# The long convolutions' transforms taken over mirrored halves of the tokens

## The chip, the cores and the metric

The kernel runs on one core of a Trainium2 chip. A time is the device time of one execution in microseconds (us). The core has TensorE (products and transposes, into PSUM), VectorE, ScalarE and GpSimd (elementwise work), and SyncE (SP), which here only issues the transfers from memory. Each engine runs its own list of instructions in order, and they meet at semaphores: an instruction can wait until a semaphore has reached a number, and raises one when it is done.

## The reference

Two transformer blocks in sequence for 256 tokens of width 1024: the first with two layers (a pooling mixer and a stick-breaking attention, each with a gated feed-forward part), the second with one layer, whose mixer has two branches, an attention over a neighbourhood and a pair of long convolutions. The change is in the convolutions alone:

```python
def long_conv_bidir(u, h_fwd, h_bwd, bias):
    B, L, C = u.shape
    k2 = jnp.concatenate([h_fwd, jnp.zeros((1, C), jnp.float32), h_bwd[:0:-1]], axis=0)
    U = jnp.fft.rfft(u.astype(jnp.float32), n=2 * L, axis=1)
    K = jnp.fft.rfft(k2, n=2 * L, axis=0)
    y = jnp.fft.irfft(U * K[None], n=2 * L, axis=1)[:, :L]
    return (y + u.astype(jnp.float32) * bias.astype(jnp.float32)).astype(u.dtype)

def hyena_mixer(hv, hx1, hx2, conv_w, conv_b, w1, b1, w2, b2, freq, w3, bias):
    u = short_conv(jnp.concatenate([hv, hx1, hx2], axis=-1), conv_w, conv_b)
    parts = jnp.split(u, HY_ORDER + 1, axis=-1)
    z, gates = parts[0], parts[1:]
    filt = hyena_filters(z.shape[1], w1, b1, w2, b2, freq, w3)
    for n in range(HY_ORDER):
        z = gates[n] * long_conv_bidir(z, filt[:, 0, n], filt[:, 1, n], bias[n])
    return z
```

Here L is 256, the width 512, and there are two convolutions in a row. All is float32.

## The kernel before

**How numbers are multiplied.** Every float32 operand of a product is split into a high and a low half (two tiles in the type float32r), and one product is three on TensorE: high by high, high by low, low by high (`mm3`). "Product" below means one of the three. For a weight tile (128 x 1024) ScalarE writes the high half (`high_halves`, L1690) and VectorE subtracts it from the tile for the low half (`low_halves`, L1002). The same pair of steps stands behind every intermediate result (`copy`, L1701, and `minus`, L1024).

**Weights.** SP loads tiles into a ring of six places; a tile's place is free when its low half is made. The halves lie in a ring of five. In the mixer, `used(n)`, written in the lists of ScalarE and VectorE, makes the halves of all tiles up to number n + 5. The order of the tiles is the list `MIX_TILES`: q0 to q3, h0 to h11 and g0 to g15, the tiles of queries, of the convolution branch and of the gates.

**The mixer's order.** It is written out by hand, once for each engine, as a list of calls. On TensorE (L850 to L920) gemms of 24 products of 256 columns (`q5`, `h_mm`, `g_mm`) stand between the attention of four pairs of heads (`na_scores`, `na_turn`, `na_attend`) and the convolution branch.

**The convolution branch.** After `h_mm(j)` ScalarE copies the result into a padded line and starts the short convolution (`h_step`), VectorE finishes it with two operations of 256 columns (`h_conv`, L1433 and L1435). For j from 0 to 7 TensorE turns the result (`h_rows`), so that tokens lie on partitions: j = 0 to 3 is the input u, 4 to 7 the first gate X1T; 8 to 11 is the second gate X2 and is not turned. `filter_tile` and `spectrum` make the filters' spectra, KS. Then, for n = 0 and 1, `transform(n)` on TensorE multiplies the 256 tokens by the cosine and the sine matrix, for each half `ft` of the frequencies and each part `c`: 2 x 2 results, each the sum over two blocks `t` of 128 tokens. VectorE multiplies them by the spectrum as complex numbers (`transform`, L1565 to L1573) and makes high and low halves with ScalarE. The way back is two more matrix products: the first return ("bt", 24 products of 512 columns) is multiplied by X1T (L1602) and becomes the input of the second transform; the second return ("bf", 48 products of 256 columns) is multiplied by X2 (L1615) and goes into the merge (`W_MIXO`), where the fourth block of the first tile waits for the last of it. One matrix serves both ways; `matrix_high` and `matrix_low` make its halves from the transfer `dft_s`.

**What stands around it.** On TensorE: `spectrum(1)`, h11, the first transform, g7, g8, g9, the first return, g10, the second transform, g11 to g14, the second return, g15, the merge. PSUM has eight banks, given out in turn; a bank waits until what it held last has been read. VectorE applies the first block's final norm to the residual (eight operations, L1609) after the second transform.

Of the kernel before, what the change touches and what calls it, by code (L numbers as in the profile page):

```python
# [13 lines left out]
KT = 8  # L14
# [45 lines left out]
def tables():  # L60
# [15 lines left out]
    a, b = np.arange(T1)[:, None], np.arange(T1)[None, :] + 0.5  # L76

    def pair(ang):
        m = np.stack([np.cos(ang), -np.sin(ang)]).astype(f32)
        return np.ascontiguousarray(m.reshape(2, 2, 128, T1).transpose(2, 0, 1, 3).reshape(128, 4 * T1))  # L80


    k = pair(2 * np.pi * a * b / 512)
    high = (k.view(np.uint32) & np.uint32(0xFFFFF000)).view(np.float32)
    o["dft_k"] = np.concatenate([high, k - high], axis=1)
    o["dft_s"] = pair(2 * np.pi * (a + 0.5) * b / 512)
# [99 lines left out]
def build(nc, T):  # L186
# [165 lines left out]
    def sems(names):  # L352
# [23 lines left out]
    mod_done, x2_u, x2_hi, x2_lo, k_cp, rope_dve, kx_hi, kx_lo, h_fin = sems(  # L376
        "mod_done x2_u x2_hi x2_lo k_cp rope_dve kx_hi kx_lo h_fin")
# [44 lines left out]
    def mix_w(step):  # L422
        return W_MIX + MIX_TILES.index(step)

# [4 lines left out]
    def tensor(pe):  # L429
# [303 lines left out]
        def h_rows(j):  # L733
            b = bank(("ht", j), u_lo if j < 4 else x1_cp, j % 4 + 1)
            pe.wait_ge(conv_done, 2 * j + 2)
            tr(pb(b, 128), f(CONV[j % 2], 128))
            tr(pb(b, 128, at=128), f(CONV[j % 2] + 128, 128)).then_inc(ht_mm, 1)
# [157 lines left out]
        pe.wait_ge(table_lo, 2)  # L895
        pe.wait_ge(u_lo, 4)
        transform(0)
        for m in range(7, 10):
# [8 lines left out]
        g_mm(10)  # L907
        pe.wait_ge(back_dve, 4)
        transform(1)
        for m in range(11, 15):  # L910
            g_mm(m)
        pe.wait_ge(dt_dve, 32)
        for j in range(4):
            b = bank(("bf", j), back_dve, 2 * j + 5)
# [1489 lines left out]
```

## Time and profile before

| | |
|---|---|
| three runs | 1004.68, 1004.76, 1005.01 us; median 1004.76 |
| the profiled execution | 1004.6 us, its span 1002.8 us |
| TensorE busy | 988.9 us, 99% |
| VectorE busy | 787.4 us, 79% |
| ScalarE busy | 556.5 us, 55% |
| granted TensorE clock | 0.998 of full on average |
| DMA | 188.02 MB, 186 GB/s read over the span |

Times within the program are counted from the span's start. Busy time of TensorE counts a product from its start to its modelled end, and products overlap, so the distance between starts says more. What the chain of waits shows is, at each step, the work that released the next. The kernel's first block ends at about 553 us, the second block's mixer runs to about 783 us, and the last feed-forward part to the end.

### The profile page before, as it was taken

The numbers are of one execution on the slowest core, as the hardware profiler recorded it, in microseconds if no ns is written. First come the engines' busy times: TensorE is split into PE (matmuls) and PEld (weight loads), VectorE is DVE, ScalarE is ACT, GpSimd is POOL, SyncE is SP. The second block draws the span as 40 slices with busy tenths as digits, with TensorE's granted clock in tenths as the row PEclk, the third lists the DMA queues.
The fourth block names the chain that finished last, engine by engine and source line by source line (L and its number), as shares of the span: only waits on it lengthen the run. The fifth ranks groups of instructions, "written<-read, shape, count | busy, mean of one in ns | idle before, by whom it ended". The sixth has DMA issues, their size and how long they took to land.

```text
span 1002.8 us, 19799 instructions
## 1 busy us (share of the span) xinstructions
PE 988.9 (99%) x7922; PEld 958.8 (96%) x7922; DVE 787.4 (79%) x1410; ACT 556.5 (55%) x932; POOL 23.1 (2%) x28
## 2 busy tenths in 40 slices
PE   9999999999999999999999999999999999999997
PEld 6999999999889999999999999999999999999997
DVE  5888889976899878989887776787788786766553
ACT  5654444444777665555454548795644565454442
POOL 4000000000000000000000000000001100000000
PEclk9999999999999999999999999999999999999999
DMA  8666667884443248886687414263334556555541
GB/s 307 217 207 225 213 216 252 288 313 145 137 132 123 95 136 316 312 271 231 212 277 248 153 43 137 100 214 130 120 108 161 181 187 204 171 192 175 162 147 42
DMA packets 53637, 188.02 MB, mean 187 GB/s; under 512 B 6120, under 2 KB 7689, under 8 KB 53034
## 3 DMA queue, kind: packets, MB, share of 16 engines
q1 hardware_dynamic: 53370, 186.17, 55.2%
q8 instruction: 63, 1.03, 0.4%
q10 hardware_dynamic: 176, 0.59, 0.2%
q14 instruction: 28, 0.23, 0.1%
HBM read 185.68 MB, written 1.05 MB: 186 GB/s over the span
## 4 chain that ended last, share of the span: by engine, by line
PE 80%; DVE 14%; ACT 3%; issue 2%; DMA 0%; DVEq 0%; POOL 0%; ACTq 0%; POOLq 0%
PE psum L445 79%; DVE memr L1002 5%; DVE memr L1024 2%; DVE memr L1209 1%; ACT memr L1690 1%; DVE mem L1206 1%; DVE mem L1200 1%; PE psum L460 1%; ACT mem L1701 1%; DMA mem<-in_w_up 0%; ACT mem L1832 0%; DVE psum L1191 0%; ACT memr L1701 0%; DVE mem L1166 0%; DVE psum L1453 0%
## 5 line engine op out<-in xcount | busy, mean ns | idle before, releaser
L445 PE MATMUL psum<-memr 128*128 128x256 f32 (+5 forms) x7666 | 957.3, 287 | 3.2 <-DVE memr L1024 1.3
L445 PEld LDWEIGHTS psum<-memr 128*128 128x128 f32 (+1 forms) x7666 | 930.6, 188 | 22.8 <-issue 7.4
L1002 DVE TENSOR_TENSOR memr<-mem,memr 128x1024 fp32r<-128x1024 f32 (+1 forms) x290 | 339.9, 1209 | 47.7 <-ACT memr L1690 47.5
L1690 ACT ACTIVATE memr<-mem 128x1024 fp32r<-128x1024 f32 (+2 forms) x296 | 290.8, 1026 | 13.2 <-DMA mem<-in_w_down 8.3
L1701 ACT ACTIVATE memr<-mem 128x256 fp32r<-128x256 f32 (+5 forms) x171 | 81.1, 484 | 282.3 <-DVE mem L1134 102.1
L1024 DVE TENSOR_TENSOR memr<-mem,memr 128x256 fp32r<-128x256 f32 (+3 forms) x129 | 59.6, 471 | 17.8 <-ACT memr L1701 16.8
L1119 DVE TENSOR_TENSOR mem<-psum,mem 128x256 f32<-128x256 f32 (+1 forms) x66 | 27.9, 423 | 42.3 <-PE psum L445 42.3
L1012 DVE CUSTOM_DVE_ANT_0 mem<-mem 128x1024 f32<-128x1024 f32 x48 | 58.6, 1221 | 0.6
L1698 ACT ACTIVATE mem<-mem 128x256 f32<-128x256 f32 (+1 forms) x56 | 22.9, 415 | 64.5 <-DVE mem L1657 32.4
L1024 DVE TENSOR_TENSOR memr<-psum,memr 128x256 fp32r<-128x256 f32 (+2 forms) x72 | 32.2, 462 | 13.5 <-ACT memr L1701 12.7
L1701 ACT ACTIVATE memr<-psum 128x256 fp32r<-128x256 f32 (+3 forms) x80 | 29.6, 404 | 7.8 <-PE psum L460 4.0
L1777 ACT ACTIVATE mem<-mem 128x256 f32<-128x256 f32 (+1 forms) x66 | 29.9, 452 | 7.0 <-DVE mem L1112 6.0
L460 PE MATMUL psum<-mem 128*128 128x128 f32 (+1 forms) x200 | 29.1, 276 | 3.4 <-DVE mem L1206 2.0
L460 PEld LDWEIGHTS psum<-mem 128*128 128x128 f32 (+1 forms) x200 | 21.6, 130 | 7.1 <-DVE mem L1206 2.5
L1112 DVE TENSOR_TENSOR mem<-psum,mem 128x256 f32<-128x256 f32 (+1 forms) x66 | 27.8, 421 | 0.1
L1701 ACT ACTIVATE mem<-psum 128x256 f32<-128x256 f32 (+2 forms) x55 | 22.3, 416 | 7.2 <-PE psum L445 6.9
L1701 ACT ACTIVATE memr<-psum,mem 16x512 fp32r<-16x512 f32 (+3 forms) x40 | 21.9, 595 | 6.9 <-PE psum L445 5.4
L1021 DVE TENSOR_TENSOR mem<-mem 128x256 f32<-128x256 f32 (+1 forms) x48 | 20.5, 427 | 4.7 <-ACT mem L1698 3.5
L1657 DVE SCALAR_TENSOR_TENSOR mem<-psum,mem 128x256 f32<-128x256 f32 x8 | 3.9, 484 | 23.3 <-PE psum L445 23.3
L1009 DVE CUSTOM_DVE_ANT_0 mem<-mem 128x1024 f32<-128x1024 f32 x16 | 19.5, 1220 | 1.4 <-ACT mem L1773 1.4
L445 PE MATMUL psum<-mem 128*128 128x512 f32 (+7 forms) x56 | 18.6, 456 | 1.7 <-POOL mem L2248 1.3
L1134 DVE TENSOR_TENSOR mem<-mem 128x272 f32<-128x272 f32 (+1 forms) x44 | 18.7, 425 | 0.3 <-ACT mem L1777 0.3
(132 smaller groups left out, 373.4 us busy)
## 6 DMA issues: line engine op xcount, KB each, us to landing
mem<-in_w_gate SPq DMA_DIRECT2D x66, 512.0 KB, 4.1
mem<-in_w_up SPq DMA_DIRECT2D x66, 512.0 KB, 4.5
mem<-in_w_ada SPq DMA_DIRECT2D x48, 512.0 KB, 4.6
mem<-in_w_down SPq DMA_DIRECT2D x48, 448.0 KB, 4.3
mem<-in_w_in SPq DMA_DIRECT2D x40, 512.0 KB, 4.4
mem<-in_w_down SPq DMA_DIRECT2D x24, 512.0 KB, 4.8
mem<-in_sb_qkv SPq DMA_DIRECT2D x24, 512.0 KB, 4.5
mem<-in_sb_o SPq DMA_DIRECT2D x8, 512.0 KB, 3.4
```

What stands on the lines that cost most here:

```text
L445: return pe.matmul(out, a, b, start=start, stop=stop)
L460: return pe.transpose(out, in_, ident[0:p, 0:p])
L1002: dve.tensor_tensor(r(ol, n), raw(e), rf(oh, n), ALU.subtract).then_inc(w_lo, 1)
L1012: dve.tensor_tensor_reduce(out=f(JUNK, 1024), in0=raw(e), in1=f(SILC, 1024), scale=1.0, scalar=0.0, op0=ALU.mult, op1=ALU.add, accum_out=f ...
L1021: dve.tensor_tensor(f(SQA, n), f(SQA, n), f(SQT[i % 2], n), ALU.add).then_inc(sq_add, 1)
L1024: return dve.tensor_tensor(out, x, hi, ALU.subtract)
L1112: last = dve.tensor_tensor(f(TT, n), pb(bg, n), f(RSTD, n), ALU.mult)
L1119: last = dve.tensor_tensor(f(UU, n), pb(bu, n), f(RSTD, n), ALU.mult)
L1690: act.activation(r(oh, n), raw(e), ACT.Copy).then_inc(w_hi, 1)
L1698: act.activation(f(SQT[i % 2] if i else SQA, n), x, ACT.Square).then_inc(sq_act, 1)
L1701: return act.activation(out, in_, ACT.Copy, bias=0.0, scale=scale)
L1777: act.activation(f(SSL, n), f(TT, n), ACT.Silu, bias=f(FCOL[k], 1) if shift else 0.0).then_inc(silu_done, 1)
```

## The change

The matrices of the transform are even or odd about the middle of the tokens, and for half of the frequencies and parts only the sum of a token and its mirror image counts, for the other half only the difference. The kernel now makes the sum and the difference (of 128 rows each) once, and each result of the transform takes one block in place of two. The frequencies are put in an order in which even ones come first. The first return gives an even part and an odd part of 128 rows, and the two halves of the tokens are their sum and their difference.

- `h_conv(j)`: for j < 4 an add and a subtract of 128 columns, of the first half and the reversed second half, into the padded line; for j 4 to 7 a reversed copy of the second half. `h_rows` turns these.
- TensorE: `transform(n)` has 12 products of 512 columns in place of 24, the first return 12 in place of 24.
- After the first return: ScalarE copies one part to SBUF; VectorE makes sum and difference, multiplies each by its part of X1T, and makes sum and difference again for the second transform.
- The matrix there and the matrix back are now different: `dft_f` (0.5 MB, already in halves) and `dft_i` (1 MB, in halves), loaded after `spectrum(1)`. ScalarE copies each into the type float32r, the second between the halves of the first transform; VectorE's `matrix_low` is gone.
- Order: on TensorE g10 now stands before the first return, g11 and g12 behind it, g13 to g15 before the second return. On VectorE the final norm stands before `h_conv(10)`, and the tiles of `used(24)` to `used(31)` are spread between other steps.

```diff
@@ tables
+    s = np.stack([np.cos(ang) + np.sin(ang), np.cos(ang) - np.sin(ang)]).astype(f32)
+    o["dft_f"] = halves(s[:, :128].transpose(1, 0, 2).reshape(128, 2 * T1))
+    o["dft_i"] = halves(s.reshape(2, T1, 2, 128).transpose(3, 0, 2, 1).reshape(128, 4 * T1))
...
@@ TensorE
+        def forward(c, ft):
+            o = MATR + 256 * c + 128 * ft
+            return r(o, 128), r(o + 512, 128)
+
+        def inverse(c, ft, n):
+            o = 512 * c + 256 * ft
+            return r(MATH + o, n), r(MATL + o, n)
...
                     b = bank(("dt", n, ft, c), dt_dve, 16 * n + 8 * ft + 2 * c + 2)
-                    for t in range(2):
-                        last = mm3(pb(b), *mat(c, t, 128 * ft, 128), r(UH + 512 * t, 512), r(UL + 512 * t, 512), t == 0, t == 1)
-                    last.then_inc(dt_mm, 1)
+                    t = (c + ft) % 2
+                    mm3(pb(b), *forward(c, ft), r(UH + 512 * t, 512), r(UL + 512 * t, 512), True, True).then_inc(dt_mm, 1)
...
-        for t in range(2):
-            b = bank(("bt", t), back_dve, 2 * t + 1)
+        pe.wait_ge(table_hi, 5)
+        for t in (1, 0):
+            b = bank(("bt", t), *((back_dve, 2), (back_cp, 1))[t])
             for c in range(2):
-                for ft in range(2):
-                    last = mm3(pb(b), *mat(c, ft, 128 * t, 128), *y_of(c, ft, 0, 512), c + ft == 0, c + ft == 2)
+                ft = (c + t) % 2
+                last = mm3(pb(b), *inverse(c, ft, 128), *y_of(c, ft, 0, 512), c == 0, c == 1)
             last.then_inc(back_mm, 1)
@@ VectorE
+            if j < 4:
+                early, late = f(CONV[k], 128), f(CONV[k] + 128, 128)[:, ::-1]
+                dve.wait_ge(conv_done, c + 2)
+                dve.tensor_tensor(f(PADB[k] + 1, 128), early, late, ALU.add).then_inc(conv_done, 1)
+                dve.tensor_tensor(f(PADB[k] + 129, 128), early, late, ALU.subtract).then_inc(conv_done, 1)
+            elif j < 8:
+                dve.wait_ge(conv_done, c + 2)
+                dve.tensor_copy(f(PADB[k] + 129, 128), f(CONV[k] + 128, 128)[:, ::-1]).then_inc(conv_done, 1)
...
+        z, x = ([f(SPARE[k] + 512 * t, 512) for t in range(2)] for k in range(2))
+        dve.wait_ge(back_mm, 2)
+        dve.wait_ge(back_cp, 1)
+        for t, op in enumerate((ALU.add, ALU.subtract)):
+            dve.tensor_tensor(z[t], pb(bank_of["bt", 0]), x[0], op).then_inc(back_dve, 1)
+        for t in range(2):
+            dve.wait_ge(back_dve, t + 1)
+            dve.tensor_tensor(z[t], z[t], f(X1T + 512 * t, 512), ALU.mult).then_inc(back_dve, 1)
+        dve.wait_ge(back_dve, 4)
+        for t, op in enumerate((ALU.add, ALU.subtract)):
+            dve.tensor_tensor(x[t], z[0], z[1], op).then_inc(back_dve, 1)
...
             dve.tensor_tensor(z, pb(bank_of["bf", j], T1), f(X2 + T1 * j, T1), ALU.mult).then_inc(back_dve, 1)
+            if j < 3:
+                used(29 + j)
@@ ScalarE
+        transform(0, 0)
+        act.wait_ge(dft_in, 48)
+        copy(r(MATH, 2048), f(MATH, 2048)).then_inc(table_hi, 1)
+        gate(7)
+        used(24)
+        transform(0, 1)
...
@@ SP
-        sp.dma_start(f(MATR, 1024), T["dft_s"]).then_inc(dft_in, 16)
+        sp.dma_start(f(MATR, 1024), T["dft_f"]).then_inc(dft_in, 16)
+        raws(W_MIX + 30)
+        sp.wait_ge(sp_mm, 8)
+        sp.dma_start(f(MATH, 2048), T["dft_i"]).then_inc(dft_in, 16)
```

TensorE before, from the third gate behind the first transform (g9) through the first return and g10 to the start of the second transform (x23 and x5 are the rest of a gemm or a result):

```order
L445 MATMUL psum<-memr 128x256 [waits ks_done,w_lo]
L445 MATMUL psum<-memr 128x256 x23
L445 MATMUL psum<-memr 128x512 [waits h_cp,dt_dve]
L445 MATMUL psum<-memr 128x512 x11
L445 MATMUL psum<-memr 128x512 [waits dt_dve]
L445 MATMUL psum<-memr 128x512 x11
L445 MATMUL psum<-memr 128x256 [waits dt_dve,w_lo]
L445 MATMUL psum<-memr 128x256 x23
L445 MATMUL psum<-memr 128x512 [waits dt_dve,back_dve]
L445 MATMUL psum<-memr 128x512 x5
```

The same place after, from g10:

```order
L454 MATMUL psum<-memr 128x256 [waits h_cp,w_lo]
L454 MATMUL psum<-memr 128x256 x23
L454 MATMUL psum<-memr 128x512 [waits dt_dve,table_hi]
L454 MATMUL psum<-memr 128x512 x5
L454 MATMUL psum<-memr 128x512 [waits dt_dve]
L454 MATMUL psum<-memr 128x512 x5
L454 MATMUL psum<-memr 128x256 [waits dt_dve,w_lo]
L454 MATMUL psum<-memr 128x256 x23
L454 MATMUL psum<-memr 128x256 [waits dt_dve,w_lo]
L454 MATMUL psum<-memr 128x256 x23
L454 MATMUL psum<-memr 128x512 [waits gate_act,back_dve]
L454 MATMUL psum<-memr 128x512 x2
```

The return has half the products, and two gemms stand between it and the second transform in place of one.

VectorE before, from the end of the first transform to the start of the second (L1002 are weight tiles, L1602 the product by the gate, L1024 low halves):

```order
L1024 TENSOR_TENSOR memr<-mem,memr 128x512 [waits y_hi] x2
L1002 TENSOR_TENSOR memr<-mem,memr 128x1024 [waits w_hi] x3
L1602 TENSOR_TENSOR mem<-psum,mem 128x512 [waits back_mm,x1_cp]
L1024 TENSOR_TENSOR memr<-mem,memr 128x512 [waits back_hi]
L1602 TENSOR_TENSOR mem<-psum,mem 128x512 [waits back_mm]
L1024 TENSOR_TENSOR memr<-mem,memr 128x512 [waits back_hi]
L1002 TENSOR_TENSOR memr<-mem,memr 128x1024 [waits w_hi]
```

The same place after:

```order
L1046 TENSOR_TENSOR memr<-mem,memr 128x512 [waits y_hi] x2
L1024 TENSOR_TENSOR memr<-mem,memr 128x1024 [waits w_hi] x2
L1633 TENSOR_TENSOR mem<-psum,mem 128x512 [waits back_cp,back_mm,x1_cp]
L1633 TENSOR_TENSOR mem<-psum,mem 128x512
L1636 TENSOR_TENSOR mem<-mem 128x512 [waits back_dve] x2
L1639 TENSOR_TENSOR mem<-mem 128x512 [waits back_dve]
L1639 TENSOR_TENSOR mem<-mem 128x512
L1046 TENSOR_TENSOR memr<-mem,memr 128x512 [waits back_hi] x2
L1024 TENSOR_TENSOR memr<-mem,memr 128x1024 [waits w_hi]
```

Eight operations stand where four stood, with one weight tile fewer ahead of them, and none of them can begin before both results are there.

VectorE after, at the third convolution tile (L1455 and L1458 are the convolution, L1462 and L1463 the two new ones) and the weights of the attention behind it:

```order
L1455 SCALAR_TENSOR_TENSOR mem<-mem 128x256 [waits h_cp]
L1458 SCALAR_TENSOR_TENSOR mem<-mem 128x256 [waits conv_done]
L1462 TENSOR_TENSOR mem<-mem 128x128 [waits conv_done]
L1463 TENSOR_TENSOR mem<-mem 128x128
L1046 TENSOR_TENSOR memr<-psum,memr 128x512 [waits pt_hi] x4
```

Before, the convolution's second operation is followed at once by the four of the attention.

## Rows read from the trace of the kernel before

**Rows 1.** The page, busy us, share of the span and instructions of an engine.
```profile
PE 988.9 (99%) x7922; PEld 958.8 (96%) x7922; DVE 787.4 (79%) x1410; ACT 556.5 (55%) x932; POOL 23.1 (2%) x28
```

**Rows 2.** The chain of waits, 726 to 1003 us: start, length, what.
```profile
726.28 267.78 PE psum L445 x2214
```

**Rows 3.** The chain of waits, 626 to 670 us.
```profile
647.73 0.48 DVE mem L1435
648.21 1.10 DVE memr L1024 x2
...
663.29 0.50 DVE mem L1433
663.81 0.49 DVE mem L1435
...
665.89 0.48 DVE mem L1435
...
669.40 0.71 PE psum L445 x2
```

**Rows 4.** TensorE's weight loads in order of time, 640 to 670 us.
```profile
653.14 1.49 PEld L445 LDWEIGHTS psum<-memr 64*128 64x128 f32 x24 [0.37 <-DVE memr L1024]
...
661.03 2.89 PEld L445 LDWEIGHTS psum<-memr 128*128 128x128 f32 x24 [0.31 <-DVE memr L1002]
```

**Rows 5.** Products by shape, 726.2 to 731.7 us: busy us, mean ns, idle.
```profile
L445 PE MATMUL psum<-memr 128*128 128x512 f32 x24 | 5.7, 395 | 0.0
```

**Rows 6.** TensorE by stretch: us, busy (starts counted), granted clock, DMA share, GB/s.
```profile
711.98:717.58 5.60, 5.60 (x26) 1.00 0.56 189
717.58:725.98 8.40, 8.40 (x74) 1.00 0.18 63
```

**Rows 7.** VectorE in order of time, 600 to 640 us: start, us.
```profile
628.77 2.48 DVE L1024 TENSOR_TENSOR memr<-psum,memr 128x512 fp32r<-128x512 f32 x4 [0.39 <-ACT memr L1701]
...
631.18 0.44 DVE L1401 STREAM_SHUFFLE mem<-mem 128x256 f32<-128x256 f32 x1
631.51 0.42 DVE L1404 TENSOR_TENSOR mem<-mem 128x256 f32<-128x256 f32 x1
631.84 0.42 DVE L1406 TENSOR_TENSOR mem<-mem 128x256 f32<-128x256 f32 x1
```

**Rows 8.** VectorE by shape, whole span.
```profile
L1206 DVE TENSOR_TENSOR mem<-mem 128x144 f32<-128x144 f32 x16 | 4.5, 284 | 0.0
```

**Rows 9.** VectorE in order of time, 705 to 735 us.
```profile
710.70 1.23 DVE L1024 TENSOR_TENSOR memr<-mem,memr 128x1024 fp32r<-128x1024 f32 x1 [4.52 <-ACT memr L1701]
...
716.16 0.68 DVE L1565 TENSOR_TENSOR mem<-psum,mem 128x512 f32<-128x512 f32 x1
716.77 0.68 DVE L1566 TENSOR_TENSOR mem<-psum,mem 128x512 f32<-128x512 f32 x1
...
721.16 0.68 DVE L1565 TENSOR_TENSOR mem<-psum,mem 128x512 f32<-128x512 f32 x1
...
730.33 0.69 DVE L1602 TENSOR_TENSOR mem<-psum,mem 128x512 f32<-128x512 f32 x1
731.72 0.69 DVE L1024 TENSOR_TENSOR memr<-mem,memr 128x512 fp32r<-128x512 f32 x1 [0.70 <-ACT memr L1701]
```

**Rows 10.** VectorE in order of time, 750 to 762 us.
```profile
754.18 3.25 DVE L1609 SCALAR_TENSOR_TENSOR mem<-mem 128x256 f32<-128x256 f32 x8
757.35 0.41 DVE L1615 TENSOR_TENSOR mem<-psum,mem 128x256 f32<-128x256 f32 x1
758.24 0.42 DVE L1024 TENSOR_TENSOR memr<-mem,memr 128x256 fp32r<-128x256 f32 x1 [0.48 <-ACT memr L1701]
```

**Rows 11.** ScalarE in order of time, 670 to 725 us.
```profile
671.65 1.98 ACT L1701 ACTIVATE memr<-mem 128x2048 fp32r<-128x2048 f32 x1
...
724.27 1.23 ACT L1701 ACTIVATE memr<-mem 128x512 fp32r<-128x512 f32 x2 [3.75 <-DVE mem L1571]
```

**Rows 12.** DMA issues, 640 to 800 us: KB each, median us to landing.
```profile
mem<-in_dft_k SPq DMA_DIRECT2D x1, 1024.0 KB, 6.9
```

More of the change, by code:

```diff
@@ L423, in mix_w, with convolved @@
         return W_MIX + MIX_TILES.index(step)
+    def convolved(j):
+        return 2 * (j + 1) + min(j + 1, 4) + min(j + 1, 8)
     bank_of = {}
@@ new lines, in transform @@
+        def transform(n, ft):
+            base, c = (SPARE, [PX[0], PX[2]])[ft], 16 * n + 8 * ft
+            t1, t2, t3, t4 = f(base[0], 512), f(base[0] + 512, 512), f(base[1], 512), f(base[1] + 512, 512)
+            kre, kim = f(KS[n] + 1024 * ft, 512), f(KS[n] + 1024 * ft + 512, 512)
+            br, bi = bank_of["dt", n, ft, 0], bank_of["dt", n, ft, 1]
+            dve.wait_ge(ks_done, 4 * n + 4)
+            dve.wait_ge(dt_mm, 4 * n + 2 * ft + 1)
+            dve.tensor_tensor(t1, pb(br), kre, ALU.mult).then_inc(dt_dve, 1)
+            dve.tensor_tensor(t3, pb(br), kim, ALU.mult).then_inc(dt_dve, 1)
+            dve.wait_ge(dt_mm, 4 * n + 2 * ft + 2)
+            dve.tensor_tensor(t2, pb(bi), kim, ALU.mult).then_inc(dt_dve, 1)
+            dve.tensor_tensor(t4, pb(bi), kre, ALU.mult).then_inc(dt_dve, 1)
+            dve.wait_ge(dt_dve, c + 3)
+            dve.tensor_tensor(t1, t1, t2, ALU.subtract).then_inc(dt_dve, 1)
+            dve.wait_ge(dt_dve, c + 4)
+            dve.tensor_tensor(t3, t3, t4, ALU.add).then_inc(dt_dve, 1)
+            for i, x in enumerate((t1, t3)):
+                o = YB + 1024 * i + 512 * ft
+                dve.wait_ge(y_hi, 4 * n + 2 * ft + i + 1)
+                minus(r(o + 2048, 512), x, rf(o, 512)).then_inc(dt_dve, 1)
@@ L1590, in vector @@
         used(20)
+        for i in range(KT):
+            dve.scalar_tensor_tensor(hx(i, NMETA, T1), hx(i, NMETA, T1), vec("final_norm", i), f(SROOT, T1),
+                                     ALU.mult, ALU.mult)
         h_conv(10)
-        matrix_low()
         used(22)
@@ L2190, in scalar @@
         used(22)
-        matrix_high()
+        act.wait_ge(dft_in, 32)
+        copy(r(MATR, 1024), f(MATR, 1024)).then_inc(table_hi, 1)
         spectrum(1)
@@ L2194, in scalar @@
         used(23)
-        transform(0)
-        for m in range(7, 10):
-            gate(m)
-            used(17 + m)
+        transform(0, 0)
+        act.wait_ge(dft_in, 48)
+        copy(r(MATH, 2048), f(MATH, 2048)).then_inc(table_hi, 1)
+        gate(7)
+        used(24)
+        transform(0, 1)
+        gate(8)
+        used(25)
+        gate(9)
+        used(26)
+        gate(10)
+        act.wait_ge(back_mm, 1)
+        copy(f(SPARE[1], 512), pb(bank_of["bt", 1])).then_inc(back_cp, 1)
         for t in range(2):
-            act.wait_ge(back_dve, 2 * t + 1)
+            act.wait_ge(back_dve, t + 5)
             act.wait_ge(dt_mm, 4)
-            copy(r(UH + 512 * t, 512), f(SPARE[t], 512)).then_inc(back_hi, 1)
-        gate(10)
+            copy(r(UH + 512 * t, 512), f(SPARE[1] + 512 * t, 512)).then_inc(back_hi, 1)
         used(27)
-        transform(1)
-        for m in range(11, 15):
-            gate(m)
-            used(17 + m)
+        gate(11)
+        gate(12)
+        transform(1, 0)
+        used(28)
+        gate(13)
+        gate(14)
+        transform(1, 1)
+        gate(15)
         for j in range(4):
-            act.wait_ge(back_dve, 2 * j + 5)
+            if j < 3:
+                used(29 + j)
+            act.wait_ge(back_dve, 2 * j + 9)
             copy(r(YHYH + T1 * j, T1), f(SPARE[j % 2] + T1 * (j // 2), T1)).then_inc(back_hi, 1)
-        gate(15)
         used(32)
```

126 lines of the change are left out of this document (49 added, 77 removed).

## The prediction, on record before the changed kernel ran

> **What bounds the kernel now.** I read the page's first part, then busy time by stretch, then the chain of waits, then each engine in order of time around the change. The page has TensorE busy for 99% of the span and VectorE for 79% [rows 1]. A busy TensorE is not proof that it sets the time, so the reader is to look at where it stops. The chain of waits after the first return is one unbroken piece of TensorE: 2214 products in 267.78 us, from 726.28 to 994.06 us [rows 2]. There, a product that is left out shortens the program by the distance between two products, and any new stop adds its full length. Before 670 us it is otherwise. The chain runs over VectorE and ScalarE for some 40 us and comes to TensorE only at 669.40 [rows 3], and TensorE's weight loads stand idle 0.37 and 0.31 us for VectorE on the way [rows 4]. So two parts of the change fall on different ground: the products fall where TensorE binds, and the folding operations fall where VectorE binds.
>
> **Products removed.** Each transform has 12 products of 512 columns in place of 24, and so does the first return; the second return keeps its 48 of 256 columns. That is 3 x 12 = 36 products. The price is the distance from start to start, not the 395 ns for which one stands busy [rows 5]: in the stretch of the first transform 26 of them (two are of 256 columns, at its edges) take 5.60 us, so 24 take 24 x 0.233; 72 of 256 columns take 8.40 us, 0.117 each, with two edge records [rows 6]. The two prices stand as 2 to 1, as the columns do. 36 x 0.233 = 8.4 us off TensorE.
>
> The Trainium skill, page "TensorE: Matmul & The Clock Gate", section "Back-to-back issue gap", says that a sustained stream of 512-column products with their weight loads runs at about 131 ns each. By that rule 36 of them would be worth 4.7 us, an estimate from the page. The trace disagrees, 233 ns against 131.
>
> **Folding on VectorE (h_conv).** Tiles 0 to 3 get an add and a subtract of 128 columns, one operand read backwards, tiles 4 to 7 one backwards copy. No row has 128 such columns. Two starts of 256-column operations are 0.33 us apart (631.18, 631.51, 631.84 [rows 7]), two of 512 columns 0.61 (716.16 and 716.77 [rows 9]), so 128 columns come to about 0.20 us. A wait on the operation just before adds some 0.12: the second operation of a convolution, which waits for the first, starts 0.52 after it (663.29 and 663.81 [rows 3]), against 0.41 where eight of the same form follow each other (3.25 us [rows 10]). So a folded tile costs 0.12 + 2 x 0.20 = 0.52 us and a copied one 0.32. Bounds: nothing where VectorE waits anyway, and 0.61 per operation if a backwards read costs as much as 512 plain columns, which is the farthest row; the 144-column row (284 ns busy, against 0.42 to 0.44 at 256 [rows 7, 8]) is the nearest, and it fits 0.20 from start to start.
> Which of them count? Tile 0 and tile 1 come before waits for ScalarE; ahead of the weights of the second pair VectorE idles 0.39 us [rows 7], so tile 1 leaves about 0.13. Tile 2 (chain at 647.73, then straight into 648.21), tile 3 (663.81) and tile 4 (665.89) are on the chain [rows 3]: 0.52 + 0.52 + 0.32. Together 1.5 us, less about 0.15 for what the ends absorb: VectorE's last piece before 669.40 is 1.35 us later. TensorE, which waited there already, has nothing left to hide it. I take +1.35, between 0 (all hidden) and 4.3 (seven operations at 0.61, and the waits). Tiles 5 to 7 fall after 670 us, where VectorE is some microseconds ahead of TensorE: nothing.
>
> From here on I use the times of the trace; the shift of 1.35 goes on top of all.
>
> **First transform.** VectorE loses matrix_low (1.23 us at 710.70, after 4.52 us of idleness) and gets the eight final_norm operations, 3.25 us, into that idleness [rows 9, 10]: hidden. It can start the complex products at about 715.5 instead of 716.16; both halves take 10.1 (716.16 to 721.16 for one [rows 9]), so they end at 725.6. TensorE ends the transform 2.8 us earlier, but the gate g10 (2.8 us) has been put behind g9, so it arrives at the return at 726.0 as before. Slack 0.4 us, cost nothing. Between the halves ScalarE gets the 2048-column copy of the return's matrix, 1.98 us; it idles 3.75 us there [rows 11], so the copy, a gate and a weight tile fit. Its data is a 1 MB transfer that SP now issues when the second spectrum is through, about 709.3 (2.8 us of h11 before 711.98); the transfer of the same size took 6.9 us [rows 12], so it lands at about 716.2 and is wanted at 719.9. SP's queue behind it (the tiles of g14 and g15 and the merge) is needed from 726 on: nothing.
>
> **First return.** This is the tightest place. Before, each half went product, ScalarE copy, subtraction, with 1.39 us from the start of the product to that of the subtraction (730.33 and 731.72 [rows 9]). Now it is add and subtract, two products by the gate, add and subtract, two ScalarE copies, two subtractions. TensorE starts its last product of the return at 728.6 and is busy with it for 0.40 [rows 5], so VectorE can begin at about 729.05; four operations at 0.60, a wait of 0.1, so the sum starts at 731.55, its low half at 732.95, the other's at 733.55, end 734.2. Gates g11 and g12 cover TensorE from 728.9 to 734.5. Slack 0.3: nothing. If that cover is gone, every 0.1 us there is 0.1 us of the total.
>
> **Second transform and return.** TensorE: transform 734.5 to 737.3, three gates to 745.7. VectorE: starts at 735.4, 5.0 for the first half, 1.14 for the weight tile between the halves, 5.05 for the second: 746.6. TensorE waits 1.0 us (before, it came with four gates and the longer transform behind it, and did not wait). Bounds: 0 (VectorE a microsecond quicker) and 2.5. I take +1.0.
> The return then ends at 752.3 and the merge's first four products at 753.7. On VectorE each tile now holds a product, a weight tile of 1.14 and a subtraction, 1.8 us against 1.4 of TensorE: the fourth subtraction ends at 755.1 (product to subtraction 0.89 [rows 10]). TensorE wants it at 754.75: +0.4. Before, g15 stood there as cover. After that both engines stand to each other as before, and nothing is left to absorb or add.
>
> **Sum.** -8.4 + 1.35 + 1.0 + 0.4 = -5.65. The profiled execution is 1004.6 us by its own clock (span 1002.8), so 998.95; the median of the runs shown is 0.16 above it: 999.1 us.
>
> **Rivals.**
> (1) The side costs hide: VectorE's folding finds idle time and the waits before the second return don't come. For it: ScalarE waits for VectorE and VectorE for ScalarE in that stretch, so the chain may have play that it doesn't show. Against: it goes from 647.73 into 648.21 without a pause [rows 3]. Time: 1004.76 - 8.4 = 996.4, with half of the costs 997.8.
> (2) The small operations are dear. Folding at 0.61 each gives +4.3 in place of 1.35, and the sum -2.7: 1002.1. The same time comes from a first return whose eight operations and two handovers outrun g11 and g12 by 3 us. For it: no row shows a backwards read, and slack is 0.3 there. Against: shuffles and strided reads have the price of plain ones (the shuffle, 0.44 busy at 256 columns [rows 7]).
> (3) Slower: the new 1 MB transfer lands late. ScalarE then stands in its order before the copy, between the two halves of the first transform; the high halves of the second half, the weight tiles and gates all queue behind it, and VectorE and TensorE wait for them. The loss is one for one after 3.7 us of slack and 0.4 of TensorE's; the gain is gone at 5.65 + 4.1 = 9.8 us late, that is a transfer of 16.7 us; at 20 us the time is 1008. For it: it shares the queues with weight tiles. Against: the worst of its kind was 6.9 us.
> (4) The page's 131 ns hold. Then -4.7 + 2.75 gives 1002.8. It is refuted by its own rows unless the folded operands stream otherwise.
>
> **Chances.** Forecast 0.65, (1) 0.14, (2) 0.14, (3) 0.04, (4) 0.03. The time is the forecast's, 999.1. Its own range is 997.6 to 1000.8; to leave out no more than 2 in 10, the range goes to 996.9 on one side, half of (1), and 1002.0 on the other, nearly all of (2). A measurement of this kernel tells 0.2%, 2 us, from no change, so faster means under 1002.75: forecast, (1), nearly all of (2), 0.91; the same 0.05; slower (3), 0.04.
>
> **What would show it.** Right: 24 products of 512 columns fewer in the two transforms and 12 in the first return, at 0.233 apart; TensorE's stop at the fourth pair's attention grows from 0.3 to over 1 us; VectorE's new operations 0.20 apart; no stop before the first return or the second transform; a stop of about 1 us before the second return and some tenths in the first merge tile. Wrong: a stop before the second transform (the first return's chain was undersized), ScalarE idle for a DMA between the halves, a lower granted clock after the new stops, or 128-column operations as long as 512-column ones.

## The result, and the profile after

| | before | after |
|---|---|---|
| median of the runs on one chip | 1004.88 us (1004.68 to 1006.58, four runs) | 999.47 us (998.78 to 999.62, four runs) |
| profiled execution | 1004.6 us, span 1002.8 | 999.62 us, span 997.8 |

The ratio is 0.9941, with an interval of 0.9924 to 0.9958: faster by 0.6%, 5.4 us between the medians and 5.0 between the spans. The forecast was 999.1.

The page of after, answering to [rows 1]:

```profile
PE 982.0 (98%) x7886; PEld 952.4 (95%) x7886; DVE 790.3 (79%) x1425; ACT 559.0 (56%) x934; POOL 23.0 (2%) x28
```

36 products fewer on TensorE, and 15 operations more on VectorE. Where they fall is seen in the stretches. The rows of after are read as those of [rows 6], with all engines in them: in each stretch first its length, then busy time and starts of PE (products), PEld (weight loads), DVE, ACT and POOL, the granted clock, the DMA share and GB/s:

```profile
714.20:717.01 2.81, 2.81 (x14) 2.30 (x14) 1.30 (x3) 2.39 (x5) 0.00 (x0) 1.00 1.00 415
717.01:728.21 11.20, 11.20 (x97) 11.16 (x96) 11.00 (x18) 6.60 (x9) 0.00 (x0) 1.00 0.35 142
728.21:730.95 2.74, 2.74 (x14) 2.30 (x13) 1.90 (x2) 2.21 (x5) 0.00 (x0) 1.00 0.37 96
730.95:736.54 5.59, 5.59 (x49) 5.55 (x48) 5.16 (x9) 2.05 (x3) 0.00 (x0) 1.00 0.40 144
736.54:739.35 2.81, 2.81 (x14) 2.31 (x14) 2.81 (x4) 0.68 (x3) 0.00 (x0) 1.00 0.26 54
```

The first row is the first transform, the third the first return, the last the second transform, each with its 12 products and an edge record or two of a neighbour: 2.81, 2.74 and 2.81 us, so 0.228 to 0.234 for a product, at a clock of 1.00. Between them lie four gates (11.20 us) and two (5.59). TensorE is busy in all of these rows, so it does not stop before the first return or before the second transform.

It stops elsewhere. TensorE's weight loads of after, in order of time, answering to [rows 4]; in brackets the idle time before a row and what ended it:

```profile
654.64 1.50 PEld L454 LDWEIGHTS psum<-memr 64*128 64x128 f32 x24 [0.76 <-DVE memr L1046]
...
662.64 2.87 PEld L454 LDWEIGHTS psum<-memr 128*128 128x128 f32 x24 [0.30 <-DVE memr L1024]
...
671.75 14.05 PEld L454 LDWEIGHTS psum<-memr 128*128 128x128 f32 x96 [1.02 <-issue]
...
700.27 47.51 PEld L454 LDWEIGHTS psum<-memr 128*128 128x128 f32 x348
748.84 8.27 PEld L454 LDWEIGHTS psum<-memr 128*128 128x128 f32 x69 [1.06 <-DVE memr L1046]
757.45 32.73 PEld L454 LDWEIGHTS psum<-memr 128*128 128x128 f32 x280 [0.34 <-DVE memr L1046]
```

Two rows of before, from the same view, that [rows 4] doesn't reach:

```profile
669.37 14.12 PEld L445 LDWEIGHTS psum<-memr 128*128 128x128 f32 x96 [0.48 <-issue]
...
726.28 63.90 PEld L445 LDWEIGHTS psum<-memr 128*128 128x128 f32 x498 [0.24 <-DVE memr L1024]
```

The stop of 0.37 at the attention of the third pair has grown to 0.76, and that of 0.48 at 669.37 to 1.02, at 671.75. Around them stand smaller ones: 0.54 at 648.43, where before had 0.44, and two of 0.19, at 656.66 and 667.63, where before had none; that of 0.31 is 0.30. All of this before 672 us adds up to 1.4 us. Two stops are new, 1.06 us before the second return and 0.34 in the first tile of the merge. And one is gone: before, TensorE waited 0.24 us for VectorE at the first return (726.28). Between 700 and 747.8 us after has no stop.

VectorE of after, in order of time, around tile 2 (the sum and the difference, L1462 and L1463) and at tile 4 (the copy, L1466):

```profile
648.81 0.48 DVE L1458 SCALAR_TENSOR_TENSOR mem<-mem 128x256 f32<-128x256 f32 x1
649.33 0.29 DVE L1462 TENSOR_TENSOR mem<-mem 128x128 f32<-128x128 f32 x1
649.54 0.28 DVE L1463 TENSOR_TENSOR mem<-mem 128x128 f32<-128x128 f32 x1
649.74 2.47 DVE L1046 TENSOR_TENSOR memr<-psum,memr 128x512 fp32r<-128x512 f32 x4
...
668.53 0.23 DVE L1466 COPY mem<-mem 128x128 f32<-128x128 f32 x1
668.68 2.35 DVE L1024 TENSOR_TENSOR memr<-mem,memr 128x1024 fp32r<-128x1024 f32 x2
```

The sum and the difference start 0.21 us apart, and the next piece 0.20 after that. One operand of each is read backwards, and they cost what the columns alone would. For that the kernel before has a row to compare with, a VectorE operation with 128 columns read forwards (its operands lie in PSUM and SBUF):

```profile
L1191 DVE TENSOR_TENSOR psum<-psum,mem 128x128 f32<-128x128 f32 x16 | 4.6, 286 | 0.0
```

It is busy for 286 ns on average, the two backwards ones for 0.29 and 0.28 us. The copy costs less: the next operation starts 0.15 us after it.

The chain of waits of after, from the fourth pair's attention on, answering to [rows 2, 3]:

```profile
671.78 14.22 PE psum L454 x96
...
700.54 30.62 PE psum L454 x216
731.24 1.29 DVE mem L1633 x2
732.53 1.21 DVE mem L1636 x2
733.77 0.70 DVE mem L1639
734.49 0.64 ACT memr L1740
735.16 1.30 DVE memr L1046 x2
736.46 1.08 DVE memr L1024
737.59 0.69 DVE mem L1591
...
742.58 1.22 DVE memr L1024
...
747.50 1.30 DVE memr L1046 x2
748.84 1.72 PE psum L454 x12
...
756.97 0.44 DVE memr L1046
757.45 42.62 PE psum L454 x363
```

Before, this was TensorE alone from 726.28 on [rows 2]. Now VectorE, with single copies of ScalarE in between, holds the chain for 17.6 us, from 731.24 to 748.84: the first return's sums, products by the gate, sums again and low halves (5.2 us), a weight tile (L1024), the complex products of one half, another weight tile at 742.58, the other half. TensorE had work beside it for all but the last 1.06 us. The second return, at 748.84, begins with 12 products of TensorE; from there the chain runs over VectorE's part of it, and after 757.45 it is TensorE's again.

TensorE's place against the kernel before can be followed by comparing the start of the same product in both traces: after 606 us it is 0.97 us later than before, at the attention of the fourth pair 2.3 later, behind the stretches above and the two stops 5.01 earlier, and so to the end. Of the 0.97, 0.89 are already there after the first 20 product records of the program, where both kernels are the same; the last section comes back to it.

### The profile page after: what moved, and what is told of

It is laid out like the page before. It is cut to its first block, busy times and chain, and to the rows that moved or that the text cites. A ratio compares the mean times of both kernels' runs of the same rounds, so it can differ in the third digit from the quotient of the medians.

```text
span 997.8 us, 19744 instructions
## 1 busy us (share of the span) xinstructions
PE 982.0 (98%) x7886; PEld 952.4 (95%) x7886; DVE 790.3 (79%) x1425; ACT 559.0 (56%) x934; POOL 23.0 (2%) x28
## 4 chain that ended last, share of the span: by engine, by line
PE 76%; DVE 16%; ACT 5%; issue 3%; DVEq 0%; POOL 0%; ACTq 0%; POOLq 0%
PE psum L454 76%; DVE memr L1024 5%; DVE memr L1046 3%; ACT mem L1740 1%; DVE memr L1231 1%; DVE mem L1228 1%; ACT memr L1729 1%; DVE mem L1222 1%; ACT mem L2058 1%; ACT memr L1740 1%; ACT mem L1871 0%; DVE psum L1484 0%; DVE psum L1213 0%; DVE mem L1188 0%; PE psum L469 0%
## 5 line engine op out<-in xcount | busy, mean ns | idle before, releaser
L1024 DVE TENSOR_TENSOR memr<-mem,memr 128x1024 fp32r<-128x1024 f32 (+1 forms) x290 | 339.1, 1206 | 43.6 <-ACT memr L1729 43.2
L1740 ACT ACTIVATE memr<-mem 128x256 fp32r<-128x256 f32 (+6 forms) x172 | 82.9, 493 | 270.7 <-DVE mem L1156 102.1
L1046 DVE TENSOR_TENSOR memr<-mem,memr 128x256 fp32r<-128x256 f32 (+4 forms) x128 | 58.3, 465 | 10.6 <-ACT memr L1740 9.6
```

Of the source, the lines that this page charges most:

```text
L1024: dve.tensor_tensor(r(ol, n), raw(e), rf(oh, n), ALU.subtract).then_inc(w_lo, 1)
L1046: return dve.tensor_tensor(out, x, hi, ALU.subtract)
L1740: return act.activation(out, in_, ACT.Copy, bias=0.0, scale=scale)
```

## The experiments

Medians in microseconds. There are three groups, each on a chip of its own, and the kernel before ran with each. With the first four experiments below it took 1005.67 (21 runs). With "The cover of the first return", "The stop before the second return", "The stop at the fourth pair's attention" and "Both, and the stop in the merge" it took 1005.25 (14). With the other four it took 1005.22 (9). The changed kernel itself ran again in the first group alone. So a difference of medians from it is inside one group there; in the other two it runs across chips, where the kernel before has moved by 0.4 us, and the ratios and the traces have to decide. Unless said otherwise a kernel is the changed one with the edit shown.

**The changed kernel again.** No edit.

> The changed kernel again, beside the others on one chip. Both theories: 0.994 to 0.995 of before. In its profile the first product starts where that of before does if the 0.8 us by which the first profile's products came later at the start is chance of the execution; 0.8 us later again if it belongs to the change.

Measured 999.45 (998.54 to 999.53), ratio 0.9935, interval 0.9922 to 0.9949, span 997.7. It is the mark for what follows. Its first row of TensorE is as long as in the first profile (11.51 us against 11.68; before 10.79).

**Without the folding.** The sums, differences and backwards copies are left out, and TensorE turns the tiles as they are; that part of the result is missing. VectorE's part of the edit:

```diff
-            if j < 4:
-                early, late = f(CONV[k], 128), f(CONV[k] + 128, 128)[:, ::-1]
-                dve.wait_ge(conv_done, c + 2)
-                dve.tensor_tensor(f(PADB[k] + 1, 128), early, late, ALU.add).then_inc(conv_done, 1)
-                dve.tensor_tensor(f(PADB[k] + 129, 128), early, late, ALU.subtract).then_inc(conv_done, 1)
-            elif j < 8:
-                dve.wait_ge(conv_done, c + 2)
-                dve.tensor_copy(f(PADB[k] + 129, 128), f(CONV[k] + 128, 128)[:, ::-1]).then_inc(conv_done, 1)
```

> The changed kernel with the folding on VectorE left out (the eight adds and subtracts and four copies in h_conv), the tokens turned unfolded; leaves out the sums and differences. Theory (the folding sits on a chain of VectorE and ScalarE that TensorE waits for at the fourth pair's attention): 1.4 us faster than the changed kernel, the last stop before 672 us back to 0.3 us. Rival (the folding hides, and the later start of the attention has another cause): no difference.

Measured 998.0 (997.17 to 998.28), ratio 0.9923, interval 0.991 to 0.9935, span 996.3: 1.45 us faster than with the folding. The weight loads show where:

```profile
653.94 1.49 PEld L454 LDWEIGHTS psum<-memr 64*128 64x128 f32 x24 [0.37 <-DVE memr L1046]
...
670.15 14.12 PEld L454 LDWEIGHTS psum<-memr 128*128 128x128 f32 x96 [0.49 <-issue]
...
747.32 8.26 PEld L454 LDWEIGHTS psum<-memr 128*128 128x128 f32 x69 [1.07 <-DVE memr L1046]
```

The stops of 0.37 and 0.49 are those of the kernel before, and the one before the second return is untouched by the folding.

**The folding alone, in the kernel before.** The block shown above is put into the kernel before, and nothing reads what it writes; who waits for the convolution now waits for it too, as in the changed kernel.

> The kernel before with the same twelve folding operations added to h_conv, their results unused, all else as before. Theory: 1.4 us slower than before (1006.2 us), shown in TensorE's stops at 653, 661 and 669 us. Rival (hidden): no difference.

Measured 1006.64 (1006.02 to 1007.8), ratio 1.0012, interval 1.0003 to 1.0021, span 1004.9: 1.0 over the kernel before by the medians, 2.1 by the spans. TensorE falls back by 1.36 us between 386 and 672 us of the program. Of the rest, 0.5 is there from the start and 0.3 comes at 383 us, where both kernels are still the same. The weight loads have the stops of after, to a few hundredths:

```profile
654.45 1.48 PEld L448 LDWEIGHTS psum<-memr 64*128 64x128 f32 x24 [0.80 <-DVE memr L1027]
...
671.55 14.05 PEld L448 LDWEIGHTS psum<-memr 128*128 128x128 f32 x96 [1.06 <-issue]
```

Taken out of one kernel and put into the other, the twelve operations cost the same: 1.3 to 1.4 us of TensorE's time, all ahead of 672 us.

**The price of a product.** Every product of the transforms and of the first return is made twice, so the 36 are back and all else is as in after.

```diff
-                    mm3(pb(b), *forward(c, ft), ...).then_inc(dt_mm, 1)
+                    for _ in range(2 if n in TWICE else 1):
+                        last = mm3(pb(b), *forward(c, ft), ...)
+                    last.then_inc(dt_mm, 1)
...
-            for c in range(2):
+            for c in (0, 1, 0, 1):
```

> The changed kernel with every product of both transforms and of the first return made twice (36 more of 512 columns), results the same. Theory (a product is worth the 0.233 us from start to start; the last transform's 2.8 us cover the 1.06 us stop before the second return): 8.4 - 1.1 = 7.3 us slower than the changed kernel. Rival (131 ns each, as the page on TensorE has it for a stream of 512 columns): 4.7 us less the stop, some 4.0 us slower.

Measured 1006.58 (1005.81 to 1007.35), ratio 1.0009, interval 1.0001 to 1.0018, span 1005.4: 7.13 over the changed kernel.

```profile
700.69 64.02 PEld L454 LDWEIGHTS psum<-memr 128*128 128x128 f32 x453
765.04 15.12 PEld L454 LDWEIGHTS psum<-memr 128*128 128x128 f32 x129 [0.34 <-DVE memr L1050]
```

The weight loads run from 700.69 to 764.7 with no stop: the one before the second return is covered. So 36 x 0.233 = 8.4, less the 1.06 that is no longer waited, is 7.3, and the 131 ns a product of the rival, which gives 4.7 - 1.06 = 3.7 (the expectation has some 4.0), is refuted by a run. It also says what the change, with its new order of gates and weight tiles, would be worth if half the products were not left out: nothing, or a small loss (1.0009).

**The cover of the first return.** The gate g12 is moved from ahead of the second transform to behind it, and ScalarE's part of it with it.

```diff
             g_mm(11)
-            g_mm(12)
             pe.wait_ge(back_dve, 8)
             transform(1)
-            for m in range(13, 16):
+            for m in range(12, 16):
```

> The changed kernel with the gate tile g12 moved from before the second transform to behind it, so that only g11 (2.8 us) covers the first return's work on VectorE and ScalarE. Theory (that work takes 5.5 us from the return's last product and the cover was exact): TensorE stops for 2.7 us before the second transform, the stop of 1.06 us before the second return goes, 1.7 us slower than the changed kernel. Rival (the cover was ample, VectorE hides it): the stop before the second return goes and nothing takes its place, 1.1 us faster.

Measured 1002.49 (1001.35 to 1003.41), ratio 0.9974, interval 0.9964 to 0.9983, span 1001.1: 3.04 over the changed kernel by the medians, from another group, and 3.2 in the traces from the stop on, where 1.7 was expected.

```profile
736.58 23.80 PEld L454 LDWEIGHTS psum<-memr 128*128 128x128 f32 x177 [2.75 <-DVE memr L1045]
```

The stop is there, with the length of one gate, and the one before the second return is gone (from 736.58 the loads run for 23.8 us). So the balance of stops is 2.75 - 1.06 = 1.7 as expected, and 1.5 us of the 3.2 are missing. They lie right behind the stop. The stretches of this kernel, as above:

```profile
730.00:736.50 6.50, 4.03 (x30) 3.63 (x28) 5.22 (x10) 2.43 (x4) 0.00 (x0) 1.00 0.49 161
736.50:740.00 3.50, 3.42 (x9) 2.68 (x10) 3.06 (x6) 0.52 (x2) 0.00 (x0) 0.55 0.37 140
740.00:745.00 5.00, 5.00 (x40) 4.80 (x39) 4.90 (x9) 2.22 (x4) 0.00 (x0) 0.97 0.02 7
```

Behind the stop TensorE's granted clock is 0.55, that is 1.2 GHz in place of 2.4 for nearly the whole stretch. Read more closely it is 1.00 through the stop and for 0.3 us after it, 0.50 from 736.9 to 740.25, and 1.00 from 740.3. What this costs can be read against the next experiment, where the clock stays at 1.00: the 177 weight loads behind the stop take 23.80 us here and 22.26 there. That is 1.5 us, which is what was missing. It is no accident of one execution: the granted clock over the whole span is 0.996 or 0.997 in all ten runs of this kernel, and 0.998 or 0.999 in every other run of this case.

**The same stop, filled.** As the kernel just told of, with 11 products of 512 columns whose result is overwritten, put where TensorE waited.

```diff
+                    if n and ft + c == 0:
+                        for _ in range(11):
+                            mm(pb(b), r(MATR, 128), r(MATR, 512), True, True)
+                        pe.wait_ge(back_dve, 8)
```

> The kernel with g12 behind the second transform (e7_g12), with 11 products of 512 columns, results unused, in TensorE's stop of 2.75 us before the second transform (11 x 0.233 = 2.56 us). Theory (of the 3.0 us that e7_g12 lost, 1.65 are stops and the rest the half clock that TensorE had for 3.4 us after the stop): the granted clock stays at 1.00 there, and the time is 1.4 us under that of e7_g12 at 1001.1 us. Rival (the 1.4 us have another cause, the clock is a bystander): the time of e7_g12, 1002.5 us.

Measured 1000.79 (1000.22 to 1001.5), ratio 0.9953, interval 0.9941 to 0.9966, span 999.0: 1.7 us faster than with the empty stop by the medians of two groups, 2.1 by the ratios and the spans, though it does 11 products more.

```profile
736.03 22.26 PEld L454 LDWEIGHTS psum<-memr 128*128 128x128 f32 x177 [0.46 <-DVE memr L1048]
```

```profile
736.50:740.00 3.50, 3.50 (x22) 3.00 (x21) 3.50 (x6) 0.00 (x0) 0.00 (x0) 1.00 0.39 150
```

The second transform starts as late as before, TensorE's idle time is 0.46 in place of 2.75, and the clock is 1.00. That separates the two parts of the price: the later start (1.7, kept) and the clock after it (1.5, gone).

**The stop before the second return.** The weight tiles 30 and 31 (counted from 0, `used(n)` ends with tile n + 4) are made earlier on VectorE: 30 where it waits for the first return's products, 31 ahead of the second transform, and none between its halves. ScalarE makes their high halves in the matching order.

```diff
@@ VectorE, ahead of the first return
-        used(25)
+        used(26)
@@ VectorE, behind it
-        used(26)
+        used(27)
         transform(1, 0)
-        used(27)
         transform(1, 1)
```

> The changed kernel with VectorE's weight tile 30 made while it waits for the first return, and tile 31 ahead of the second transform in place of between its halves. Theory (the stop of 1.06 us before the second return is VectorE's 1.14 us of a weight tile between the halves): that stop is gone or under 0.1 us, 1.1 us faster than the changed kernel. Rival (the stop comes from the complex products themselves, or moves on to the merge): the stop in the first merge tile grows by as much, no gain.

Measured 998.75 (997.42 to 999.54), ratio 0.9935, interval 0.9923 to 0.9948, span 996.2. Only one stop is left behind 672 us:

```profile
755.82 34.37 PEld L454 LDWEIGHTS psum<-memr 128*128 128x128 f32 x294 [0.33 <-DVE memr L1046]
```

The 1.06 are gone. TensorE is about 1.1 us earlier for it in the trace, besides 0.6 that this execution has from its start. By the medians the gain is 0.7, across two groups; by the ratio to the kernel before, 0.9935 in both, there is none. The size rests on the trace alone.

**The stop at the fourth pair's attention.** The weight tiles 15 and 16 are made behind the halves of the attention weights that TensorE waits for, and not ahead of them; on ScalarE likewise.

```diff
-        used(12)
         weights_low(3)
+        used(12)
```

> The changed kernel with two weight tiles (15 and 16) made behind the fourth pair's attention weights in place of before them, on ScalarE and VectorE. Theory (TensorE waits at the fourth pair's attention for a VectorE that is busy with tiles not yet wanted): the stop of about 1 us there goes, 1 us faster than the changed kernel; what stops before it (0.4 to 0.6 us in all) stay. Rival (the chain is bound by ScalarE or TensorE's transposes there): under 0.3 us.

Measured 997.61 (996.76 to 998.21), ratio 0.9925, interval 0.9913 to 0.9938, span 995.8.

```profile
666.65 2.87 PEld L454 LDWEIGHTS psum<-memr 128*128 128x128 f32 x24 [0.19 <-DVE memr L1024]
...
746.84 8.27 PEld L454 LDWEIGHTS psum<-memr 128*128 128x128 f32 x69 [1.06 <-DVE memr L1046]
```

The 1.02 at 671.75 are gone, the later stops stay. The median is 1.8 us lower, across two groups, and the ratio 0.0010, that is 1.0 us. In the trace 1.1 us is this, and 0.9 lies at the start of the program.

**Both, and the stop in the merge.** Both edits, and the third weight tile among the merge's subtractions is made behind the last low half.

```diff
-            if j < 3:
+            if j < 2:
                 used(29 + j)
```

> Both edits together, and weight tile 35 behind the second return's last low half. Theory (the three stops are separate, each given back in full): 1.0 + 1.1 + 0.3 = 2.4 us faster than the changed kernel. Rival (the stops move on): less than 1.5 us.

Measured 996.36 (995.89 to 997.2), ratio 0.9914, interval 0.9901 to 0.9928, span 994.1.

```profile
698.09 91.98 PEld L454 LDWEIGHTS psum<-memr 128*128 128x128 f32 x728
```

TensorE's weight loads run from 698 to 790 us without a stop. Comparing the traces gives 2.7 us for the three places (1.02 + 1.06 + 0.34 = 2.4 as stops). The ratio gives 2.1 us, the medians across two groups 3.1.

**The transfer of the return's matrix.** SP issues the 1 MB transfer when the last result of the first transform is through TensorE, about 5 us later.

```diff
-        sp.wait_ge(sp_mm, 8)
+        sp.wait_ge(dt_mm, 4)
```

> The changed kernel with the 1 MB transfer of the return's matrix held back until the first transform's last result (dt_mm at 4) in place of the second spectrum's, so that it is issued about 5.7 us later, near 717.4 us, and lands near 722.1 to 724. The changed kernel's ScalarE wants it at 721.9. Theory (the prediction's third rival: slack at ScalarE, then one for one): 0 to 2 us slower, TensorE's stop before the first return as long as the landing is late less 0.4 us. Rival (the landing has more play, since ScalarE idles 0.7 us behind the copy): no difference.

Measured 999.19 (998.78 to 999.85), ratio 0.9938, interval 0.9926 to 0.9951: no difference. The issue in order of time, and ScalarE's copies, among them that of the matrix:

```profile
716.75 0.33 SPq L2385 DMA_DIRECT2D mem<-in_dft_i  x1
```

```profile
720.38 3.07 ACT L1740 ACTIVATE memr<-mem 128x512 fp32r<-128x512 f32 x3 [4.28 <-DVE mem L1597]
```

Issued at 716.75 it took 4.8 us and landed at 721.5, and ScalarE's three operations, the last of them the copy of the matrix, took 3.07 us as they do in after, where the issue is at 711.63 and the same piece reads 3.04. So the transfer has at least 5.1 us to spare in after. It landed just in time here, so what a transfer that is really late costs was not seen.

**The kernel before, a second profile.** No edit.

> The kernel before once more, for its profile. The first product that counts came 0.8 us later in the changed kernel's profile, and between 0.0 and 1.0 us later in those of its variants, whose beginnings are the same. If that is chance of an execution, this profile's start may differ from the first of the same kernel by some tenths; if it belongs to each built program, it is the same within 0.1 us.

Measured 1004.57, a single execution, span 1002.7. Its first row of TensorE is 10.26 us long, against 10.79 in the first profile of the same kernel. So half a microsecond there is not fixed by the built program.

**The best version again.** The edits of "Both, and the stop in the merge".

> The kernel with both edits of the weight tiles again, on the chip of this job, beside before: 0.991 to 0.992 of before, and the same three stops gone. Its start in the profile tells as that of b0_before does.

Measured 997.09 (995.8 to 997.74), ratio 0.9916, interval 0.9902 to 0.9929, span 994.0. With the first time of it: 0.8% faster than the kernel before, and 2 to 3 us faster than the change (2.1 and 1.9 by the ratios, 3.1 and 2.4 by the medians).

## Why the prediction was right, by its own steps

**Products, -8.4.** Held. The stretches of after have 12 products in 2.74 to 2.81 us, and putting the 36 back costs 7.1 by the medians, inside one group, against 7.3 expected with the stop that they cover.

**Folding, +1.35.** Held: 1.45 by leaving it out, 1.36 in the trace by adding it to the kernel before. Its working held too: 0.52 us for a folded tile is what the trace has (649.74, where the next operation would have started at about 649.2). Where a size was off, it was that of the copies: 0.15 in place of 0.20. Three readings were wrong without harm. "No row has 128 such columns" and "no row shows a backwards read" overlook L1191, with 128 columns forwards, and the scans of L1200, which read and write backwards. The bound of 4.3 is seven operations at 0.61 alone; with the four waits of 0.12 it would be 4.8. And the stop at the fourth pair's attention, taken as 0.3, was 0.48 before.

**Stop before the second return, +1.0.** 1.06. That it is made by the weight tile between the two halves of the complex products is shown by the run that makes it elsewhere.

**Stop in the first merge tile, +0.4.** 0.34, shown by the run in which it is gone.

**First return, 0.** Held, and narrow: VectorE's eight operations and two handovers took 5.2 us from 731.24 to 736.46, forecast 5.15, and the second transform's first product stands at 736.59, 0.12 behind the last of g12 like any other, so that the slack was nearer to 0.1 than to 0.3. The sentence that every 0.1 us without this cover is 0.1 of the total fell: with the cover taken away the stop cost 2.75, and the clock behind it some 1.5 more. So rival (2), a first return that outruns its cover by 3 us, would, by an estimate from that run, have come out near 1003.6 and not at 1002.1.

**First transform and the transfer, 0.** No new stop; the final norm's eight operations (3.25 us) cost nothing that shows, and the transfer took 4.7 us with at least 5.1 to spare. Rival (3), which reckoned with 6.9 us and 3.7 to spare, had less room than there was, and even so nothing that it needs. One term was missed. TensorE "arrives at the return at 726.0 as before", but before it then waited 0.24 us for VectorE (the row at 726.28). That wait is gone, as the prediction's own times have it (VectorE done at 725.6), so the term is -0.24 and not 0.

**The rivals.** (1), that the side costs hide, is refuted by the stops themselves, one by one, and by the two folding runs. (4), 131 ns a product, is refuted by the doubled products. The Trainium skill, page "TensorE: Matmul & The Clock Gate", section "Back-to-back issue gap", has that figure for 512 columns with their weight loads. The traces of this case disagree, with 228 to 234 ns at full clock, before and after, folded operands or not.

**What was not foreseen.** The sum of the terms with their measured sizes is -8.4 + 1.4 + 1.06 + 0.34 - 0.24 = -5.8, and the profiled execution gained 5.0. At the start of the program the profiled execution of after had 0.9 us more before its first 20 product records were through, which brings the sum to -4.9. So the forecast, with -5.65, was good in each of its terms, but that the total came within 0.4 us of the median is in part luck: the missed 0.24 and the start, which is no part of the change as far as the traces show (below), lie on opposite sides.

## What to carry to other kernels

Price work that is left out by the distance from start to start, and only where the chain of waits is one unbroken piece of that engine; then go through each handover whose cover has become shorter, because shortening the work of the bound engine by 8.4 us made two new stops of 1.4 in all. Such stops were taken away again by moving weight tiles that nobody waited for behind the operation that somebody waited for, with no operation removed. And a stop is not priced by its length alone: 1.06 us cost 1.06, while 2.75 us cost 4.3, since the clock fell behind it.

## What the runs showed of the hardware

**The clock after a stop.** After 2.75 us without work TensorE ran at 1.2 GHz for about 3.4 us (a granted clock of 0.50 between 736.9 and 740.25), beginning 0.3 us after it had resumed. After the stops of 1.02 and 1.06 us the clock stayed at 1.00. What lies between the two was not tried. Eleven products without use, put into the stop, kept the clock and made the kernel 1.7 us faster by the medians.

**Reading backwards.** A VectorE operation of 128 columns of float32 with one operand read backwards is busy for 0.28 to 0.29 us, as one that reads forwards (286 ns, L1191 of before), and lets the next start after 0.20 to 0.21; a backwards copy is busy for 0.23 and lets it start after 0.15.

**The start of the program.** The first row of TensorE is 10.26 to 11.85 us long over the 14 traces of this case, though all kernels begin the same way. It holds the 20 records of ten products without use (the loop over `NWARM`), which wait for one memset of GpSimd and for nothing else. In the kernel before and in after:

```profile
1.31 10.79 PE L445 MATMUL psum<-mem 128*128 128x512 f32 x20 [1.31 <-POOL mem L2248]
```

```profile
1.31 11.68 PE L454 MATMUL psum<-mem 128*128 128x512 f32 x20 [1.31 <-POOL mem L2295]
```

Two executions of one kernel differ by 0.2 to 0.5 us there (before 10.79 and 10.26, after 11.68 and 11.51, the best version 10.81 and 10.57). The changed kernel's are longer than those of the kernel before and of the best version, but its variants, which all begin the same way, spread over 10.49 to 11.85. The weight loads of these products show where the time goes, first before, then after:

```profile
4.89 0.34 PEld L445 LDWEIGHTS psum<-mem 128*128 128x128 f32 x1 [0.52 <-issue]
5.50 0.19 PEld L445 LDWEIGHTS psum<-mem 128*128 128x128 f32 x1 [0.28 <-issue]
```

```profile
6.59 0.34 PEld L454 LDWEIGHTS psum<-mem 128*128 128x128 f32 x1 [0.52 <-issue]
7.25 0.19 PEld L454 LDWEIGHTS psum<-mem 128*128 128x128 f32 x1 [0.32 <-issue]
```

Up to 4.89 in before and 6.59 in after a weight load takes 0.34 us and the products start 0.85 us apart; from 5.50 and 7.25 on a load takes 0.19 and the products start 0.43 apart. Twice the pace is the step from 1.2 to 2.4 GHz, and the trace's own record of a full clock begins at 5.25 us in before and at 7.04 in after (before these moments there is no record). The 1.79 us between them, spent at half the pace, are the 0.89 us by which after is late. It is so in all 14 traces: the full clock begins between 4.2 and 7.4 us, and the row is longer by half of what it comes later. Since it differs by 0.3 to 1.1 us between two executions of one kernel, a difference between the spans of two single traces is sure here only to about a microsecond, and stops and terms are better compared within a trace. What sets the moment was not tried, and a part of the change in it is not excluded.
